# Expert weights in a mixture-of-experts stage: 96 transfers of 4 MB instead of 192 of 2 MB

## The chip, the cores and the metric

One core of one Trainium2 chip runs the whole program in one launch. The metric is the device time in microseconds of one execution; lower is better. All data is float32.

## What is computed

The reference is two network blocks, one after the other, on 256 tokens of width 1024. The first block mixes tokens with a long convolution and a gated linear scan, then runs a two-level mixture of experts. The second has two layers with five branches each (attention, recurrences, gated mixing, attention to a memory) and a wide merge. The change lies in the mixture of experts, whose core is, for every expert:

```python
def hier_moe(h, w_rg, w_re, w_gate, w_up, w_down):
    ...
    def expert_block(args):
        xe, e = args
        return (jax.nn.silu(xe @ w_gate[e]) * (xe @ w_up[e])) @ w_down[e]
    yb = lax.map(expert_block, (xb, block_eid)).reshape(n_slots, D)
    y = jnp.zeros_like(hf).at[tok_buf].add(yb * gate_buf[:, None].astype(yb.dtype))
```

There are 64 experts, of which each token uses two. One expert has a gate and an up matrix of 1024 x 512 and a down matrix of 512 x 1024. A weight is used for the few tokens that its expert gets, so all 64 experts' weights, 403 MB, have to be read once.

## The kernel before

The expert stage runs in rounds; in a round each expert takes up to 32 tokens (CAP). The 192 fetches of the profile are one round: 16 groups (NGRP) of 4 experts (GRP), 12 units to a group. A unit is 2 MB, 16 KB on each of 128 partitions (WSLOT is 4096 floats). Units 0 to 3 of a group hold the gate weights, 4 to 7 the up weights, 8 to 11 the down weights. They go through the tile `ring`, six slots of one unit (RING): unit v goes to slot (v + 2) % 6.

SyncE (SP) does nothing but wait and issue DMAs. `expert_unit` waits until the counter `unit_free` says that the slot is free, and issues the fetch of a unit; it is called 12 times for the first group and 12 times per turn of a loop for the others. `unit_free` is raised by 4 at L1405 and by 2 at L1409, when the first stage has left slots 2 to 5 and then 0 and 1, and after that by TensorE (PE) by one after the last matmul of each unit. Each slot has a semaphore of its own, `w2_in0` to `w2_in5`, for its arrivals. Behind the expert fetches in the same queue, SP issues the first three units of the next block's weights (L445), each when its slot is free.

TensorE runs, for each group:

- L1443: gathers the group's tokens by matmuls with one-hot matrices (L1880, L1884 on VectorE prepare them); L1447 are two transposes that ScalarE copies (L1588). VectorE copies the gathered tokens to `xg` (L1889).
- L1456: for each unit v of 0 to 7, a wait for the unit, then its 8 matmuls, which show as 16 records in the profile. ScalarE (L1590) and VectorE (L1891 to L1893) work on the gate product after unit 3.
- L1461: after VectorE has made `mid` (L1896), four transposes, which ScalarE copies (L1592).
- L1470: for each unit v of 8 to 11, a wait, then its matmuls. VectorE copies the result (L1899).
- L1475: scatters the result back; VectorE adds it to the tokens (L1903), and the next group's one-hot matrices follow.

What lies between the end of unit 11 and the start of the next group's unit 0 is called the boundary below; TensorE uses no weights in it. After the last group come the final norm (L243, L1913), a barrier of all engines (L1915) and the second block, whose first matmuls are L511.

Of the kernel before, what the change touches and what calls it, by code (L numbers as in the profile page):

```python
# [13 lines left out]
P = 128  # L14
# [17 lines left out]
NGRP = NE // GRP  # L32
# [13 lines left out]
WSLOT = 4096  # L46
LN_EXP = "natural_log_exp_and_others"
RING = 6
# [204 lines left out]
def build_program(nc, d, spot):  # L253

    with ExitStack() as ctx:
# [8 lines left out]
        ring = ctx.enter_context(nc.sbuf_tensor("ring", [P, RING, WSLOT], F32))  # L264
# [936 lines left out]
        def _(sp):  # L1201
# [16 lines left out]

            def expert_unit(v, g, free):

                s = (v + 2) % RING
                sp.wait_ge(sem("unit_free"), free + v + 1)
                src = d["w_experts"][bass.ds(g * 12 + v, 1), :, :].rearrange("a p n -> (a p) n")
                sp.dma_start(ring[:, s, :], src).then_inc(sem(f"w2_in{s}"), 16)


            for v in range(12):
                expert_unit(v, 0, 0)
            sp.wait_ge(sem("rounds"), 1)
            n_rounds = sp.value_load(rounds[0:1, 0:1], min_val=1, max_val=SEQ // CAP)  # L1230
            with sp.Fori(1, n_rounds * NGRP) as it:
                g = sp.snap(it % NGRP)
                for v in range(12):
                    expert_unit(v, g, it * 12)
            for u in range(RING2):
# [5 lines left out]
        def _(pe):  # L1241
# [195 lines left out]
            with pe.Fori(0, n_rounds) as r:  # L1437
                with pe.Fori(0, NGRP) as g:
# [11 lines left out]
                    for v in range(8):  # L1450
                        s = (v + 2) % RING
                        pe.wait_ge(sem(f"w2_in{s}"), it * 32 + (v // RING + 1) * 16)
                        w = ring[:, s, :].rearrange("p (k e n) -> p k e n", k=2, n=FE)
                        for k in range(2):
                            for e in range(GRP):
                                last = pe.matmul(ps[CAP * e:CAP * (e + 1), v // 4, :], xg[:, (v % 4) * 2 + k, CAP * e:CAP * (e + 1)],  # L1456
                                                 w[:, k, e, :], start=(v % 4 == 0 and k == 0), stop=(v % 4 == 3 and k == 1))
                        last.then_inc(sem("unit_free"), 1)
# [5 lines left out]
                    for v in range(8, 12):  # L1464
                        s = (v + 2) % RING
                        pe.wait_ge(sem(f"w2_in{s}"), it * 32 + (v // RING + 1) * 16)
                        w = ring[:, s, :].rearrange("p (e n) -> p e n", n=D)
# [486 lines left out]
def expert_units(gate, up, down):  # L1954
# [4 lines left out]
    out[:, 8:] = np.asarray(down).reshape(NGRP, GRP, 4, P, D).transpose(0, 2, 3, 1, 4).reshape(NGRP, 4, P, WSLOT)  # L1959
    return out.reshape(NGRP * 12, P, WSLOT)  # L1960

# [71 lines left out]
```

## Time and profile before

| | us |
|---|---|
| median of 3 runs | 2566.71 |
| lowest and highest | 2566.13, 2588.36 |
| the profiled execution | 2564.53 |
| its span | 2562.8 |
| TensorE matmul busy | 2143.2 (84%) |
| VectorE busy | 911.7 (36%) |
| q1, the queue of SP's DMAs | 585.45 MB in 43672 packets, 56.7% of 16 engines |

The profiled execution took 1.73 us more than its span; the span is what the trace covers, from the first instruction to the last. Its own time lies 2.18 us below the median of the runs. The expert stage lies between about 440 and 1397 us of the span. A row of the timeline merges consecutive instructions of one line on one engine. "PE ... [1.47 <-DMA ring<-in_w_experts]" says that TensorE sat idle for 1.47 us before this row until a fetch of expert weights had landed. SPq is SyncE's instruction queue.

### The profile page before, as it was taken

The numbers are of one execution on the slowest core, as the hardware profiler recorded it, in microseconds if no ns is written. First come the engines' busy times: TensorE is split into PE (matmuls) and PEld (weight loads), VectorE is DVE, ScalarE is ACT, GpSimd is POOL, SyncE is SP. The second block draws the span as 40 slices with busy tenths as digits, with TensorE's granted clock in tenths as the row PEclk, the third lists the DMA queues.
The fourth block names the chain that finished last, engine by engine and source line by source line (L and its number), as shares of the span: only waits on it lengthen the run. The fifth ranks groups of instructions, "written<-read, shape, count | busy, mean of one in ns | idle before, by whom it ended". The sixth has DMA issues, their size and how long they took to land. (4 is left out here: it accounts for less than half of the span.)

```text
span 2562.8 us, 25793 instructions
## 1 busy us (share of the span) xinstructions
PE 2143.2 (84%) x10250; PEld 1416.8 (55%) x10250; DVE 911.7 (36%) x1500; ACT 290.7 (11%) x650; POOL 0.2 (0%) x4
## 2 busy tenths in 40 slices
PE   6997988667666666656666999999998999999998
PEld 3583466322222222223222777778887777868887
DVE  4245452211211111121121335455553235455553
ACT  1111021000000000000001222111002122111001
POOL 0000000000000000000000000000000000000000
PEclk7997777778888888888888999999999999999999
DMA  5130005799999999999997333324445333224442
GB/s 218 66 132 1 0 1 218 335 429 423 428 429 428 428 428 429 428 428 429 429 428 320 131 132 132 113 77 172 148 148 192 138 132 126 97 98 155 160 154 82
DMA packets 45198, 592.18 MB, mean 231 GB/s; under 512 B 5463, under 2 KB 6904, under 8 KB 7928
## 3 DMA queue, kind: packets, MB, share of 16 engines
q1 hardware_dynamic: 43672, 585.45, 56.7%
q10 hardware_dynamic: 1440, 5.57, 0.6%
q8 instruction: 55, 0.90, 0.1%
q14 instruction: 31, 0.25, 0.0%
HBM read 589.95 MB, written 1.05 MB: 231 GB/s over the span
## 5 line engine op out<-in xcount | busy, mean ns | idle before, releaser
L484 PE MATMUL ps<-arena,ring 128*128 128x256 f32 x1920 | 433.8, 382 | 7.9 <-DVE arena L911 7.8
L484 PEld LDWEIGHTS ps<-arena,ring 128*128 128x128 f32 x1920 | 362.4, 191 | 61.6 <-DVE arena L911 9.1
L1456 PE MATMUL ps<-ring,arena 128*32 128x512 f32 x2048 | 261.8, 658 | 111.9 <-DMA ring<-in_w_experts 92.1
L691 PE MATMUL ps<-arena,ring 128*128 128x256 f32 x1280 | 289.2, 378 | 0.0
L1470 PE MATMUL ps<-ring,arena 128*32 128x512 f32 x1024 | 179.0, 834 | 107.6 <-DMA ring<-in_w_experts 100.8
L691 PEld LDWEIGHTS ps<-arena,ring 128*128 128x128 f32 x1280 | 241.8, 189 | 35.3 <-issue 1.0
L1456 PEld LDWEIGHTS ps<-ring,arena 128*32 128x32 f32 x2048 | 65.0, 116 | 290.7 <-issue 148.2
L1470 PEld LDWEIGHTS ps<-ring,arena 128*32 128x32 f32 x1024 | 33.5, 133 | 236.6 <-DMA ring<-in_w_experts 156.9
L1250 PE MATMUL ps<-arena,ring 128*128 128x272 f32 (+1 forms) x640 | 150.6, 398 | 2.3 <-DVE arena L1731 2.3
L697 PE MATMUL ps<-arena,ring 128*128 128x256 f32 x640 | 151.6, 378 | 0.0
L1443 PE MATMUL ps<-arena 128*128 128x128 f32 x512 | 89.4, 356 | 67.2 <-DVE arena L1884 67.2
L1113 DVE RECIPROCAL arena<-arena 128x256 f32<-128x256 f32 x80 | 140.3, 1754 | 3.0 <-DVE arena L1112 0.3
L1250 PEld LDWEIGHTS ps<-arena,ring 128*128 128x128 f32 x640 | 124.0, 194 | 31.0 <-issue 5.6
L697 PEld LDWEIGHTS ps<-arena,ring 128*128 128x128 f32 x640 | 121.0, 189 | 17.5
L1899 DVE COPY arena<-ps 128x512 f32<-128x512 f32 x32 | 20.6, 688 | 300.9 <-PE ps L1470 300.9
L1443 PEld LDWEIGHTS ps<-arena 128*128 128x128 f32 x512 | 86.4, 267 | 73.4 <-DVE arena L1884 73.4
L1112 DVE TENSOR_SCALAR arena<-arena 128x256 f32<-128x256 f32 x80 | 23.7, 296 | 176.1 <-ACT arena L876 176.1
L1475 PE MATMUL ps<-arena 128*128 128x256 f32 x256 | 65.9, 415 | 22.5 <-DVE arena L1899 22.5
L497 PE MATMUL ps<-ring,arena 128*128 128x512 f32 x192 | 84.2, 593 | 0.0
L1475 PEld LDWEIGHTS ps<-arena 128*128 128x128 f32 x256 | 51.7, 207 | 51.4 <-DVE arena L1899 43.6
L876 ACT ACTIVATE arena<-ps 128x256 f32<-128x256 f32 x80 | 30.9, 386 | 371.9 <-PE ps L691 371.9
L908 DVE RECIPROCAL arena<-arena 128x256 f32<-128x256 f32 x40 | 70.2, 1755 | 1.4
(347 smaller groups left out, 1802.7 us busy)
## 6 DMA issues: line engine op xcount, KB each, us to landing
ring<-in_w_experts SPq DMA_DIRECT2D x192, 2048.0 KB, 25.5
ring<-in_w_layers SPq DMA_DIRECT2D x44, 2048.0 KB, 7.8
ring<-in_w_layers SPq DMA_DIRECT2D x40, 1536.0 KB, 6.5
ring<-in_w_first SPq DMA_DIRECT2D x10, 2048.0 KB, 8.5
arena<-in_late ACTq DMA_DIRECT2D x2, 896.0 KB, 4.9
arena<-in_fourier SPq DMA_DIRECT2D x1, 1632.0 KB, 13.8
arena<-in_gm_rows ACTq DMA_DIRECT2D x2, 768.0 KB, 6.3
arena<-in_const SPq DMA_DIRECT2D x1, 1141.0 KB, 5.2
```

What stands on the lines that cost most here:

```text
L484: last = pe.matmul(ps[:, j % 2, 0:SEQ], t[:, s, k, :], lhs[:, k, :], start=(k == 0), stop=(k == KD - 1))
L497: last = pe.matmul(ps[:, bank_of(name, j), :], lhs[:, k, m * P:(m + 1) * P], t[:, :, k, :], start=(k == 0), stop=(k == KD - 1))
L691: last = pe.matmul(ps[:, j % 2, 0:SEQ], t[:, k, :], an[:, k, :], start=(k == 0), stop=(k == KD - 1))
L697: last = pe.matmul(ps[:, (j + 1) % 2, 0:SEQ], t[:, KD + k, :], y_all[:, n, k, :], start=(k == 0), stop=(k == 3))
L876: act.activation(esig[:, p % 2, :], ps[:, j % 2, 0:SEQ], ACT.Exp, scale=-1.0).then_inc(sem(f"job_out{j % 2}"), 1)
L908: link(dve.reciprocal(e, e))
L1113: link(dve.reciprocal(e, e))
L1250: last = pe.matmul(ps[:, j % 2, 0:n], w[:, s, k, :], rhs(k), start=(k == 0), stop=(k == KD - 1))
L1443: last = pe.matmul(ps[:, 4 + k // 4, (k % 4) * P:(k % 4 + 1) * P], xn[:, tt, k * P:(k + 1) * P], onehot[:, tt, :], start=(tt == 0), stop=( ...
L1456: last = pe.matmul(ps[CAP * e:CAP * (e + 1), v // 4, :], xg[:, (v % 4) * 2 + k, CAP * e:CAP * (e + 1)], w[:, k, e, :], start=(v % 4 == 0 a ...
L1470: last = pe.matmul(ps[CAP * e:CAP * (e + 1), 2 + half, :], mid_t[:, v - 8, CAP * e:CAP * (e + 1)], w[:, e, half * 512:(half + 1) * 512], s ...
L1475: last = pe.matmul(ps[:, 4 + k // 2, (k % 2) * SEQ:(k % 2 + 1) * SEQ], y_slot[:, k * P:(k + 1) * P], back, start=True, stop=True)
```

## The change

The host lays two consecutive units side by side for each partition: the array is 96 blocks of 128 x 8192 in place of 192 of 128 x 4096. `expert_pair` replaces `expert_unit`: it is called for v = 0, 2, ... 10, waits until both slots of the pair are free (free + v + 2 in place of free + v + 1) and fetches 4 MB into the adjoining slots s and s + 1, 32 KB on each partition. Three semaphores remain, `w2_in0` to `w2_in2`, one for each pair of slots. TensorE waits only ahead of the even units. Its matmuls, their order, the ring's 96 KB per partition and the rise of `unit_free` by one after each unit stay as they are.

```diff
--- before.py
+++ after.py
@@ -1216,22 +1216,22 @@
                     sp.wait_ge(sem("strip"), 4 * (u - RING1 + 1))
                 sp.dma_start(ring[:, u % RING1, :], d["w_first"][u]).then_inc(sem(f"w1_in{u % RING1}"), 16)
 
-            def expert_unit(v, g, free):
+            def expert_pair(v, g, free):
 
                 s = (v + 2) % RING
-                sp.wait_ge(sem("unit_free"), free + v + 1)
-                src = d["w_experts"][bass.ds(g * 12 + v, 1), :, :].rearrange("a p n -> (a p) n")
-                sp.dma_start(ring[:, s, :], src).then_inc(sem(f"w2_in{s}"), 16)
-
-
-            for v in range(12):
-                expert_unit(v, 0, 0)
+                sp.wait_ge(sem("unit_free"), free + v + 2)
+                src = d["w_experts"][bass.ds(g * 6 + v // 2, 1), :, :].rearrange("a p n -> (a p) n")
+                sp.dma_start(xr(ring[:, s:s + 2, :]), src).then_inc(sem(f"w2_in{s // 2}"), 16)
+
+
+            for v in range(0, 12, 2):
+                expert_pair(v, 0, 0)
             sp.wait_ge(sem("rounds"), 1)
             n_rounds = sp.value_load(rounds[0:1, 0:1], min_val=1, max_val=SEQ // CAP)
             with sp.Fori(1, n_rounds * NGRP) as it:
                 g = sp.snap(it % NGRP)
-                for v in range(12):
-                    expert_unit(v, g, it * 12)
+                for v in range(0, 12, 2):
+                    expert_pair(v, g, it * 12)
             for u in range(RING2):
                 sp.wait_ge(sem("unit_free"), n_rounds * (NGRP * 12) + (SLOT2[u] - 2) % RING + 1)
                 layer_unit(sp, 0, u)
@@ -1449,7 +1449,8 @@
                     pe.wait_ge(sem("xg"), 2 * it + 2)
                     for v in range(8):
                         s = (v + 2) % RING
-                        pe.wait_ge(sem(f"w2_in{s}"), it * 32 + (v // RING + 1) * 16)
+                        if v % 2 == 0:
+                            pe.wait_ge(sem(f"w2_in{s // 2}"), it * 32 + (v // RING + 1) * 16)
                         w = ring[:, s, :].rearrange("p (k e n) -> p k e n", k=2, n=FE)
                         for k in range(2):
                             for e in range(GRP):
@@ -1463,7 +1464,8 @@
                     pe.wait_ge(sem("mid_t"), it + 1)
                     for v in range(8, 12):
                         s = (v + 2) % RING
-                        pe.wait_ge(sem(f"w2_in{s}"), it * 32 + (v // RING + 1) * 16)
+                        if v % 2 == 0:
+                            pe.wait_ge(sem(f"w2_in{s // 2}"), it * 32 + (v // RING + 1) * 16)
                         w = ring[:, s, :].rearrange("p (e n) -> p e n", n=D)
                         for half in range(2):
                             for e in range(GRP):
@@ -1957,7 +1959,7 @@
     for i, w in enumerate((gate, up)):
         out[:, 4 * i:4 * i + 4] = np.asarray(w).reshape(NGRP, GRP, 4, 2, P, FE).transpose(0, 2, 4, 3, 1, 5).reshape(NGRP, 4, P, WSLOT)
     out[:, 8:] = np.asarray(down).reshape(NGRP, GRP, 4, P, D).transpose(0, 2, 3, 1, 4).reshape(NGRP, 4, P, WSLOT)
-    return out.reshape(NGRP * 12, P, WSLOT)
+    return out.reshape(NGRP * 6, 2, P, WSLOT).transpose(0, 2, 1, 3).reshape(NGRP * 6, P, 2 * WSLOT)
 
 
 def layout(a):
```

On SyncE, the first group's fetches and the head of the loop over the others (`-` before, `+` after; ISA is a wait):

```order
 L1217 DMA ring<-in_w_first 128x4096 [waits strip] x6
-L1224 DMA ring<-in_w_experts 128x4096 [waits unit_free] x12
+L1224 DMA ring<-in_w_experts 128x8192 [waits unit_free] x6
 L1230 TENSOR_LOAD rounds [waits rounds]
 L1230 ISA x2
@@ -19,38 +19,20 @@
 L1231 ISA
 L1224 ISA [waits unit_free]
-L1224 DMA ring<-in_w_experts 128x4096
+L1224 DMA ring<-in_w_experts 128x8192
 L1222 REGISTER_ALU
 L1224 ISA [waits unit_free]
```

The twelve fetches of 128 x 4096 ahead of the loop are six of 128 x 8192, and in the loop each wait stands ahead of a fetch of twice the size; the loop shrinks from twelve such steps to six.

On TensorE, the down units 8 to 11 of a group, before:

```order
L1470 MATMUL ps<-ring,arena 32x512 [waits w2_in4,mid_t]
L1470 MATMUL ps<-ring,arena 32x512 x7
L1470 MATMUL ps<-ring,arena 32x512 [waits w2_in5]
L1470 MATMUL ps<-ring,arena 32x512 x7
L1470 MATMUL ps<-ring,arena 32x512 [waits w2_in0]
L1470 MATMUL ps<-ring,arena 32x512 x7
L1470 MATMUL ps<-ring,arena 32x512 [waits w2_in1]
L1470 MATMUL ps<-ring,arena 32x512 x7
```

and after (line numbers have moved by two):

```order
L1472 MATMUL ps<-ring,arena 32x512 [waits w2_in2,mid_t]
L1472 MATMUL ps<-ring,arena 32x512 x15
L1472 MATMUL ps<-ring,arena 32x512 [waits w2_in0]
L1472 MATMUL ps<-ring,arena 32x512 x15
```

Four waits, one ahead of each unit's matmuls, have become two, and unit 9 follows unit 8, and unit 11 unit 10, with no wait between them. (The program counts 8 matmuls to a unit, the profile 16 records.)

## Rows read from the trace of the kernel before

**Rows 1.** Page, part 2: GB/s moved in each of 40 slices of 64 us.
```profile
GB/s 218 66 132 1 0 1 218 335 429 423 428 429 428 428 428 429 428 428 429 429 428 320 131 132 132 113 77 172 148 148 192 138 132 126 97 98 155 160 154 82
```

**Rows 2.** Page, part 5: the matmuls that use the expert units, gate/up and down.
```profile
L1456 PE MATMUL ps<-ring,arena 128*32 128x512 f32 x2048 | 261.8, 658 | 111.9 <-DMA ring<-in_w_experts 92.1
...
L1470 PE MATMUL ps<-ring,arena 128*32 128x512 f32 x1024 | 179.0, 834 | 107.6 <-DMA ring<-in_w_experts 100.8
```

**Rows 3.** DMA view, 600 to 1300 us: packets and what they moved.
```profile
DMA packets 20594, 299.93 MB, mean 428 GB/s; under 512 B 2288, under 2 KB 2288, under 8 KB 2288
...
q1 hardware_dynamic: 20594, 299.93, 100.6%
```

**Rows 4.** Waits of the DMA-issuing queue: total us, times, longest.
```profile
SPq L1224 <- PE ps L1456: 554.8, 126, 37.6
...
SPq L1224 <- PE ps L1470: 259.0, 60, 6.0
```

**Rows 5.** Line 1224, its DMAs: issue to landing.
```profile
DMA to landing us min/median/max: 7.7/25.5/27.2
```

**Rows 6.** Timeline at the start: start us, us, engine, line, operation, count, [idle before].
```profile
458.83 10.51 PE L1456 MATMUL ps<-ring,arena 128*32 128x512 f32 x96 [1.25 <-DVE arena L1889]
...
460.81 59.33 SPq L1224 DMA_DIRECT2D ring<-in_w_experts  x16
```

**Rows 7.** Timeline at the end of the expert stage.
```profile
1370.38 3.33 PE L1470 MATMUL ps<-ring,arena 128*32 128x512 f32 x16 [2.13 <-DMA ring<-in_w_experts]
...
1375.27 1.93 PE L1470 MATMUL ps<-ring,arena 128*32 128x512 f32 x16 [1.56 <-DMA ring<-in_w_experts]
...
1399.31 2.92 PE L511 MATMUL ps<-ring 128*128 128x512 f32 x3 [7.62 <-ACT ring L745]
```

**Rows 8.** Timeline of the boundary between groups 9 and 10.
```profile
1018.01 3.43 PE L1470 MATMUL ps<-ring,arena 128*32 128x512 f32 x16 [2.97 <-DMA ring<-in_w_experts]
...
1022.90 1.93 PE L1470 MATMUL ps<-ring,arena 128*32 128x512 f32 x16 [1.47 <-DMA ring<-in_w_experts]
...
1026.24 3.72 PE L1475 MATMUL ps<-arena 128*128 128x256 f32 x16 [1.41 <-DVE arena L1899]
...
1034.17 5.46 PE L1443 MATMUL ps<-arena 128*128 128x128 f32 x32 [4.21 <-DVE arena L1884]
...
1041.10 4.49 PE L1456 MATMUL ps<-ring,arena 128*32 128x512 f32 x39 [1.24 <-DVE arena L1889]
```

**Rows 9.** Timeline of the boundary between groups 1 and 2.
```profile
553.02 3.64 PE L1470 MATMUL ps<-ring,arena 128*32 128x512 f32 x16 [1.25 <-DMA ring<-in_w_experts]
...
558.08 6.78 PE L1475 MATMUL ps<-arena 128*128 128x256 f32 x16 [1.41 <-DVE arena L1899]
...
576.97 4.50 PE L1456 MATMUL ps<-ring,arena 128*32 128x512 f32 x40 [1.24 <-DVE arena L1889]
```

**Rows 10.** Windows: busy us (count) of PE, PEld, DVE, ACT, POOL, PEclk, DMA, GB/s.
```profile
545.00:564.00 19.00, 14.54 (x54) 5.96 (x47) 1.29 (x2) 0.00 (x0) 0.00 (x0) 0.50 1.01 429
...
1039.00:1052.00 13.00, 9.65 (x88) 3.23 (x87) 4.39 (x4) 0.97 (x2) 0.00 (x0) 1.00 1.01 431
```

**Rows 11.** Waits of VectorE at the boundaries, 400 to 1360 us.
```profile
DVE arena L1889 <- PE ps L1443: 90.9, 16, 6.5
...
DVE arena L1903 <- PE ps L1475: 64.7, 15, 6.9
```

**Rows 12.** DMA view, 1398 to 1412 us: small packets alone.
```profile
DMA packets 576, 2.11 MB, mean 151 GB/s; under 512 B 64, under 2 KB 192, under 8 KB 576
...
q10 hardware_dynamic: 576, 2.11, 40.8%
```

**Rows 13.** DMA view, 14 to 34 us: packets of mixed size, back to back.
```profile
DMA packets 671, 8.60 MB, mean 430 GB/s; under 512 B 74, under 2 KB 74, under 8 KB 148
...
q1 hardware_dynamic: 671, 8.60, 101.8%
```

## The prediction

> **What bounds the kernel now.** I read four views. First, the page's slices of moved bytes [rows 1]: from slice 9 on, for twelve slices of 64 us, the core moves 423 to 429 GB/s, and nowhere else as much. That plateau is the expert stage. Second, the page's groups [rows 2]: TensorE's unit matmuls (L1456, L1470) are busy 261.8 and 179.0 us in all, and sat idle 92.1 and 100.8 us ahead of them until a fetch had landed. So TensorE waits for weights, not the other way round. Third, the DMA view of 700 us inside the plateau [rows 3]: the 16 engines' packets fill 100.6% of their time. No engine pauses, so in this stage the end is set by bytes and by time per byte. Fourth, SyncE's waits [rows 4]: it stands still until TensorE frees a slot, 126 and 60 times, yet the engines never run dry, since about five older fetches are in flight: a fetch lands 25.5 us (median) after its issue [rows 5], and one follows another by 4.89 us (1370.38 to 1375.27, [rows 7]).
>
> The stream runs from the first refill, issued at 460.81 [rows 6], to the last landing at about 1375.2 [rows 7]: 186 units (192 less the six fetched in advance) in 914 us. After it comes a serial tail to the second block's first matmul at 1399.31 [rows 7], which moves with it.
>
> **The change, part by part.** The bytes stay. Changed are the size of a packet, the moment at which a fetch may start, and the moment at which TensorE may begin.
>
> 1. Packets. A partition's row is one packet: [rows 3] has 20594 packets less 2288 completion markers, 18306 for 299.93 MB, which is 16.4 KB each. With rows of 32 KB, each of 16 engines moves 8 packets for 4 MB where it moved 16, so 8 fixed costs per pair go, in 93 streamed pairs. The trace has no 32 KB packet. From one side: in [rows 12], 512 data packets of 4.1 KB take 0.408 x 16 x 14 us = 91.4 us, 178 ns each; in [rows 3], 1.006 x 16 x 700 us / 18306 = 615 ns each. The slope is 437 ns over 12.26 KB, and the line meets zero bytes at 32 ns. This is too high for a stream, because transfers that start from rest are in it. It bounds the gain at 93 x 8 x 32 ns = 24 us. From the other side: in [rows 13], back to back, 597 data packets averaging 14.4 KB moved 430 GB/s, no less than the 428 of full 16 KB rows, so nothing is seen to be lost to packets: gain 0. The stream resembles the second far more, so I take a quarter of the first, 8 ns: 6.0 us gained. A loss from larger rows is a rival below.
>
> The Trainium skill's "DMA: Bandwidth & Descriptors" (Where 436 GB/s comes from) gives the fabric's ceiling as 435 GB/s; the 428 of [rows 3] are 1.6% below it. If all of that were fixed cost per packet, an estimate from that page, halving the packets would give back 0.8% of 914 us, 7.5 us, in place of 6.0. Packets of 32 KB are not in the trace.
>
> 2. Start. SyncE now waits for two freed units. 96 records, six units, take 10.51 us [rows 6], 1.75 us a unit at the full clock. The first refill goes out after the second unit in place of the first: +1.7 us. The stream has no slack to take it back. The four units issued ahead (L1405) and the two behind (L1409) were free at the same moments anyway.
>
> 3. End. Unit 10 was consumed while unit 11 was under way; now both land together. TensorE starts 32 records after the last landing in place of 16. One unit costs 1.75 us at full clock and 3.3 to 3.6 us at half [rows 7, 9]: +1.7 to +3.5, I take +2.5. The next block's first fetches, queued on SyncE behind the experts, also wait for units 6, 10 and 11 of the last group. The last of these is freed 2 us after the last landing and a lone 2 MB takes 7.7 us [rows 5], so the first is there well before the 1399.31 of L511, and later ones are needed later: 0.
>
> 4. The boundary between groups is the place at risk. While TensorE is between unit 11 and the next group's unit 1, only the fetches in flight feed the engines. Let pair 5 (units 10, 11) land at time 0. Pairs 0, 1 and 2 of the next group then last for 3 x 9.79 = 29.4 us. The next fetch goes into pair 0's slots, so TensorE must have finished unit 1 of the next group before that, less the time from a freed slot to moving bytes. For this time 7.7 us for a lone fetch less 4.9 us of transfer gives at most 2.8 us [rows 5, 7]. Between groups 9 and 10 [rows 8], from the start of unit 11 at 1022.90 to unit 0 at 1041.10 are 18.2 us, plus two units, 3.7 us: 21.9. Pairing adds unit 10 in front, 1.7 to 3.3 us: 23.6 to 25.2. With 2.8 that is 26.4 to 28.0, inside 29.4: no stall. Between groups 1 and 2 [rows 9] it is 23.95 + 3.7 = 27.6, with unit 10 29.3 to 30.9, and with the latency up to 33.7: a stall of 0 to 4.3 us, I take 1.9. The difference is TensorE's clock. In [rows 10] the slow boundary's first part is at a granted 0.50, which is 1.2 GHz, and a later stretch at 1.00, 2.4 GHz; the scatter took 6.78 us against 3.72 [rows 8, 9]. How many boundaries are slow? VectorE's waits [rows 11] average 64.7/15 = 4.31 us for the scatter and 90.9/16 = 5.68 for the gather, against 3.88 and 5.56 at the fast one (its matmul time plus about 0.1). Summed, that is about 8 us of excess, of which the slow boundary has 4. So I count one stalled boundary of 15: +1.9.
>
> In the kernel before, the same six units in flight, 29.4 us, stood against a shorter chain, which ended with unit 0: 18.2 + 1.9 = 20.1 us, or 25.9 at the slow boundary [rows 8, 9]. That is why [rows 1] shows no dip there.
>
> Inside a group TensorE consumes a pair in 3.5 to 7 us of each 9.79, so it is never behind, and the two waits removed per pair save nothing while it waits for the same bytes. SyncE issues half as many fetches of about 0.3 us each; it was idle: 0.
>
> Sum: -6.0 + 1.7 + 2.5 + 1.9 = +0.1 us. On the profiled execution that is 2564.53 + 0.1 = 2564.6. That run lies 2.2 us below the median of runs, 2566.71; on the median it is 2566.8, my forecast.
>
> **The rivals.**
>
> - Larger rows bring nothing per byte, because the descriptors are cut to 16 KB again or their fixed cost is hidden. The change then doesn't do what it says for the packets. For it: [rows 13]. Against it: the slope of [rows 12]. Then -6.0 falls away: 2566.8 + 6.0 = 2572.8.
> - Every boundary stalls (the other side). TensorE's work is the same, but comes in bursts after gaps of 4 to 6 us, where it was spread in gaps of 3. If it enters every boundary at 1.2 GHz, the 15 chains look like [rows 9]: 15 x 1.9 = 28.5 us in place of 1.9, which gives 2593.4. It decides from the point where the chain plus latency passes 29.4 us. For it: units already take 3.4 us after a gap of 2.97 us [rows 8]. Against it: in that same row the chain was fast all the same, and the scatter after it ran at 3.72.
> - The rate falls. 16 engines read rows that lie 32 KB apart in place of 16 KB; if their reads met in the memory more often, the plateau itself would sink. Each percent costs 9.1 us; 3% give 2566.8 + 27.4 = 2594.2. Nothing in the trace shows it. The same page of the Trainium skill (Latency and other measured facts) reports copies with power-of-two row pitches losing rate, 207 GB/s at a pitch of 512 KiB and 103 at 4 MiB, with 214 as the full rate; no row here has such a pitch.
> - The fixed cost is really the 32 ns of [rows 12]: -24 in place of -6.0, 2548.8.
>
> **How the numbers follow.** The forecast has 0.69, no gain per packet 0.15, all boundaries 0.08, a falling rate 0.03, the large gain 0.03, and 0.02 are for what I did not think of. About 1% (26 us) is what a measurement of this kernel can tell from no change. Faster by over 1% would need more than the whole upper bound of the gain: 0.02. Slower by over 1% takes the second or third rival, of which a tenth may be milder: 0.10. Within 1%: 0.88. The range: below, 12 ns a packet (3.0 less), no stall (1.9 less), an end at full clock (0.8 less) and the profiled run's lower base (2.2 less) give 2558.9, say 2558. Above, no gain per packet (6.0 more), three boundaries stalled in place of one (3.8 more) and an end at half clock (1.0 more) give 2577.6, say 2578.
>
> **What would show it.** In the profile after: q1 with 12288 data packets and 1536 completion markers fewer (about 29850 in place of 43672), each expert row as one packet of about twice the duration; a plateau of 428 to 431 GB/s; the first refill at about 462.5; the last landing near 1373 and L511 at about 1399.4; TensorE's idle time before L1457 and L1472 in half as many pieces of twice the length. A DMA share under 100% in any stretch of the plateau is a boundary stall, with one pair's fetch landing more than 9.8 us after the one before. It would be wrong if the packets stay at 16 KB, if the rate drops, or if dips come in every group.

## The result, and the profile after

The changed kernel is slower, by about half a percent. Over 20 runs of each, the ratio of its runs to those of the kernel before is 1.0053, with a 95% interval of 1.0028 to 1.0079; the medians are 2597.94 and 2583.98 us. The runs of either kernel lie at two levels 18 to 20 us apart, for a reason ahead of the expert stage (last section), so times are compared here level with level: lower level 2580.2 against 2566.7 in the mean (7 and 6 runs), upper level 2600.2 against 2584.9. That is +13.5 and +15.3 us. The profiled execution took 2579.68 us, its span is 2577.9, against 2564.53 and 2562.8. The forecast was +0.1, on a median of three runs (2566.71) that equals the mean of the lower six, and its range ended at 2578.

| | before | after |
|---|---|---|
| profiled execution, us | 2564.53 | 2579.68 |
| first unit's matmul | 458.83 | 458.57 |
| first refill issued | 460.81 | 462.27 |
| last landing used by TensorE | 1375.27 | 1385.78 |
| second block's first matmul | 1399.31 | 1414.45 |
| expert stage, first unit to second block | 940.5 | 955.9 |

The whole loss lies in the expert stage: +15.4 us there, +15.1 in the span.

The page of the changed kernel: GB/s in 40 slices, the packets of q1, and the two groups of unit matmuls. They answer to [rows 1] and [rows 2].

```profile
GB/s 217 65 131 1 0 1 217 348 424 416 427 418 429 422 428 430 416 430 427 422 422 298 160 131 112 99 109 150 159 157 168 160 131 111 98 110 150 158 158 82
...
q1 hardware_dynamic: 29848, 585.45, 56.3%
...
L1457 PE MATMUL ps<-ring,arena 128*32 128x512 f32 x2048 | 261.2, 667 | 132.5 <-DMA ring<-in_w_experts 112.6
...
L1472 PE MATMUL ps<-ring,arena 128*32 128x512 f32 x1024 | 171.9, 832 | 111.8 <-DMA ring<-in_w_experts 111.8
```

q1 has 29848 packets, as was expected of 32 KB rows. The twelve slices of the plateau, 423 to 429 in [rows 1], now run from 416 to 430: some are as high as before and some lower. TensorE's idle time ahead of the unit matmuls until a fetch had landed rose from 92.1 + 100.8 to 112.6 + 111.8 us.

The DMA view of the changed kernel for the same 700 us as in [rows 3]. Its GB/s row has 40 slices of 17.5 us.

```profile
GB/s 421 448 410 427 442 403 433 427 440 376 442 419 423 431 438 412 418 433 429 421 433 431 410 438 431 434 374 446 423 418 423 444 418 421 436 433 389 446 423 403
DMA packets 10196, 296.88 MB, mean 424 GB/s; under 512 B 1136, under 2 KB 1136, under 8 KB 1136
...
q1 hardware_dynamic: 10196, 296.88, 99.3%
```

The mean fell from 428 to 424 GB/s and the engines' share from 100.6% to 99.3%: they now pause. In the fine row the low values (410, 403, 376, 374, 389) come back about once in three or four slices, once to a group.

The timeline at both ends of the stage, which answers to [rows 6] and [rows 7]:

```profile
458.57 10.51 PE L1457 MATMUL ps<-ring,arena 128*32 128x512 f32 x96 [1.25 <-DVE arena L1891]
...
462.27 7.20 SPq L1224 DMA_DIRECT2D ring<-in_w_experts  x3
...
1385.78 6.57 PE L1472 MATMUL ps<-ring,arena 128*32 128x512 f32 x32 [6.00 <-DMA ring<-in_w_experts]
...
1414.45 5.95 PE L511 MATMUL ps<-ring 128*128 128x512 f32 x8 [7.61 <-ACT ring L745]
```

The first refill goes out 3.7 us after the first matmul, in place of 2.0: the late start of 1.7 us, as predicted. From the last landing to the second block are 28.67 us in place of 24.04: a late end of 4.6 us, where 2.5 were predicted.

The boundary between groups 0 and 1, which answers to [rows 8]:

```profile
495.55 6.24 PE L1472 MATMUL ps<-ring,arena 128*32 128x512 f32 x32 [4.28 <-DMA ring<-in_w_experts]
...
503.21 3.72 PE L1477 MATMUL ps<-arena 128*128 128x256 f32 x16 [1.42 <-DVE arena L1901]
...
511.18 5.40 PE L1443 MATMUL ps<-arena 128*128 128x128 f32 x32 [4.25 <-DVE arena L1886]
...
518.04 10.51 PE L1457 MATMUL ps<-ring,arena 128*32 128x512 f32 x96 [1.24 <-DVE arena L1891]
...
536.51 0.20 PEld L1457 LDWEIGHTS ps<-ring,arena 128*32 128x32 f32 x8 [8.87 <-DMA ring<-in_w_experts]
```

Units 10 and 11 landed at 495.55, and unit 1 of the next group was done at about 518.04 + 3.64 = 521.7, so the chain is 26.1 us long, 0.9 above the 23.6 to 25.2 predicted for a boundary at full clock. Yet the refill, pair 3, was usable only at 536.51, which is 40.96 us after pair 5. Four transfers at 9.71 us (a sixth of 58.28, the group without dips measured below) take 38.85. The stream lost 2.1 us. Windows around this boundary and the next show where (busy us of the engines, then the granted TensorE clock, the DMA share, GB/s; a packet is counted, with its time and its bytes, in the window in which it starts):

```profile
515.00:521.00 6.00, 4.76 (x45) 2.53 (x47) 1.29 (x2) 0.37 (x1) 0.00 (x0) 1.00 1.00 431
521.00:523.00 2.00, 2.00 (x24) 0.67 (x20) 0.00 (x0) 0.00 (x0) 0.00 (x0) 1.00 0.97 328
523.00:525.00 2.00, 2.00 (x24) 0.59 (x20) 0.00 (x0) 0.00 (x0) 0.00 (x0) 1.00 0.62 229
525.00:531.00 6.00, 3.55 (x36) 0.87 (x28) 4.48 (x3) 0.60 (x1) 0.00 (x0) 1.00 1.01 431
...
581.00:583.00 2.00, 2.00 (x24) 0.58 (x20) 0.00 (x0) 0.00 (x0) 0.00 (x0) 1.00 0.08 33
```

Up to 521 the engines run at 431 GB/s. Then follow 328 and 229, with a share of 0.62 in the last, and at 525 all run again. From 521 to 523 the share is still 0.97 at only 328 GB/s, so the packets that start there take about a quarter longer than those before. At the next boundary two microseconds hold 33 GB/s. A dip stands in every one of the 15 boundaries, but they are unequal in depth.

VectorE's waits in the boundaries, as in [rows 11]:

```profile
DVE arena L1891 <- PE ps L1443: 98.6, 16, 6.9
...
DVE arena L1905 <- PE ps L1477: 62.1, 16, 3.9
```

62.1/16 = 3.9 us for the scatter says that TensorE's clock was at 2.4 GHz in all 16 scatters. The slow boundary on which the prediction laid its whole stall did not come back; the stalls came without it.

A measure that needs no ends: from the landing of units 10 and 11 of group 0 (495.55) to that of group 15 (1385.78) are 15 groups of 59.35 us. Before, unit 11 landed at 494.29 and 1375.27: 58.73 us a group. I call this the group period below; where units 10 and 11 land one after the other it is taken from unit 11. Before, every group takes 58.7 or 58.8 us. In the changed kernel single groups take 58.3 to 60.4 us, and 59.35 is their mean.

### The profile page after: what moved, and what is told of

Its sections match the earlier page's. It is cut to its first block and busy times, and to the rows that moved or that the text cites. A ratio compares the mean times of both kernels' runs of the same rounds, so it can differ in the third digit from the quotient of the medians.

```text
span 2577.9 us, 25427 instructions
## 1 busy us (share of the span) xinstructions
PE 2129.9 (83%) x10250; PEld 1428.8 (55%) x10250; DVE 912.0 (35%) x1500; ACT 290.7 (11%) x650; POOL 0.2 (0%) x4
## 3 DMA queue, kind: packets, MB, share of 16 engines
q1 hardware_dynamic: 29848, 585.45, 56.3%
HBM read 589.95 MB, written 1.05 MB: 229 GB/s over the span
## 5 line engine op out<-in xcount | busy, mean ns | idle before, releaser
L1457 PE MATMUL ps<-ring,arena 128*32 128x512 f32 x2048 | 261.2, 667 | 132.5 <-DMA ring<-in_w_experts 112.6
L1472 PE MATMUL ps<-ring,arena 128*32 128x512 f32 x1024 | 171.9, 832 | 111.8 <-DMA ring<-in_w_experts 111.8
L1457 PEld LDWEIGHTS ps<-ring,arena 128*32 128x32 f32 x2048 | 69.5, 121 | 312.7 <-issue 176.7
L1472 PEld LDWEIGHTS ps<-ring,arena 128*32 128x32 f32 x1024 | 43.4, 145 | 229.1 <-issue 142.4
L1443 PE MATMUL ps<-arena 128*128 128x128 f32 x512 | 97.1, 376 | 67.2 <-DVE arena L1886 67.2
L1113 DVE RECIPROCAL arena<-arena 128x256 f32<-128x256 f32 x80 | 140.3, 1754 | 3.0 <-DVE arena L1112 0.3
L697 PEld LDWEIGHTS ps<-arena,ring 128*128 128x128 f32 x640 | 121.0, 189 | 17.5
L1477 PE MATMUL ps<-arena 128*128 128x256 f32 x256 | 59.5, 385 | 22.7 <-DVE arena L1901 22.7
L1898 DVE TENSOR_TENSOR arena<-arena,ps 128x512 f32<-128x512 f32 x16 | 11.0, 690 | 178.0 <-PE ps L1457 178.0
```

The source lines that it names most:

```text
L697: last = pe.matmul(ps[:, (j + 1) % 2, 0:SEQ], t[:, KD + k, :], y_all[:, n, k, :], start=(k == 0), stop=(k == 3))
L1113: link(dve.reciprocal(e, e))
L1443: last = pe.matmul(ps[:, 4 + k // 4, (k % 4) * P:(k % 4 + 1) * P], xn[:, tt, k * P:(k + 1) * P], onehot[:, tt, :], start=(tt == 0), stop=( ...
L1472: last = pe.matmul(ps[CAP * e:CAP * (e + 1), 2 + half, :], mid_t[:, v - 8, CAP * e:CAP * (e + 1)], w[:, e, half * 512:(half + 1) * 512], s ...
L1477: last = pe.matmul(ps[:, 4 + k // 2, (k % 2) * SEQ:(k % 2 + 1) * SEQ], y_slot[:, k * P:(k + 1) * P], back, start=True, stop=True)
```

## The experiments

Theory A: the queues run dry at every boundary, because with pairs the first refill after it needs unit 10, unit 11, the boundary, unit 0 and unit 1 one after the other. Theory B: rows of 32 KB, or the layout that goes with them, are slower by themselves. Theory A2: one of the two coarse waits is enough by itself. For each kernel the table gives the stage (first unit's matmul to the second block's first, from the timeline), the group period, the mean rate from 600 to 1300 us, and the ratio to the kernel before with its interval.

| kernel | stage us | group period us | GB/s | ratio to before |
|---|---|---|---|---|
| before | 940.5 | 58.73 | 428 | |
| after | 955.9 | 59.35 | 424 | 1.0053 (1.0028 to 1.0079) |
| e_both | 959.4 | 59.67 | 421 | 1.0081 (1.0048 to 1.0114) |
| e_sp_pair | 943.7 | 58.76 | 428 | 1.0016 (0.9986 to 1.0046) |
| e_pe_pair | 944.7 | 58.77 | 428 | 1.0015 (0.9987 to 1.0043) |
| e_layout | 941.8 | 58.73 | 428 | 0.9997 (0.9968 to 1.0025) |
| e_after_twice | 990.4 | 61.45 | 410 | 1.0209 (1.0157 to 1.0262) |
| e_before_twice | 947.5 | 58.97 | 426 | 1.0032 (0.9997 to 1.0067) |
| e_split | 937.5 | 58.44 | 431 | 0.9989 (0.9960 to 1.0018) |
| e_split6 | 939.0 | 58.37 | 431 | 1.0001 (0.9979 to 1.0023) |
| e_split10 | 936.3 | 58.37 | 431 | 0.9995 (0.9964 to 1.0026) |
| e_hoist | 938.0 | 58.28 | 432 | 1.0014 (0.9987 to 1.0041) |
| e_hoist_before | 940.1 | 58.72 | 429 | 0.9977 (0.9952 to 1.0002) |
| e_hoist_split10 | 935.7 | 58.36 | 431 | 0.9916 (0.9886 to 0.9946) |

Most differences here are smaller than the spread of the runs, so the stage and the period decide; each is read from one profiled run.

**The waits without the large transfer (e_both).** The kernel before with both waits made coarse; layout and fetches of 2 MB stay.

```diff
-                sp.wait_ge(sem("unit_free"), free + v + 1)
+                sp.wait_ge(sem("unit_free"), free + v + 2 - v % 2)
...
-                        pe.wait_ge(sem(f"w2_in{s}"), it * 32 + (v // RING + 1) * 16)
+                        if v % 2 == 0:
+                            pe.wait_ge(sem(f"w2_in{s}"), it * 32 + (v // RING + 1) * 16)
+                            pe.wait_ge(sem(f"w2_in{s + 1}"), it * 32 + (v // RING + 1) * 16)
```

> The kernel before with its layout and its 2 MB fetches of 16 KB rows, but SyncE waits for both slots of a pair ahead of the first of its two fetches, and TensorE waits for both units of a pair ahead of the first. Theory A (the queues run dry at each boundary, since the chain from the landing of a pair to the freeing of the next pair's slots is too long): the same dips as in the changed kernel, about 0.6 us of idle engines and as much of slow restart in each of 15 boundaries, and without the gain of larger packets: 2564.5 + 13.6 + 6 = about 2584, last landing near 1391. Rival B (32 KB rows or the layout are slower by themselves): no loss but the later start and end, 2564.5 + 4 = 2569.

Measured: 2581.97 us in the profiled run, stage 959.4, period 59.67, units 10 and 11 of the last group in use at 1388.56. The DMA view, 600 to 1300 us:

```profile
GB/s 430 429 407 432 428 422 432 427 429 425 432 427 403 433 428 409 428 432 428 390 431 426 404 430 432 427 400 433 426 411 433 430 390 423 430 426 368 432 432 398
DMA packets 20252, 294.86 MB, mean 421 GB/s; under 512 B 2256, under 2 KB 2256, under 8 KB 2256
```

The same dips without any 32 KB row: ten slices between 368 and 411, and none that low in between. The loss against before is 18.9 us of stage, more than the changed kernel's 15.4, since the larger packets are missing. Theory B is not needed for the dips, and e_hoist below rules it out. The size of the step from this kernel to the changed one is 3.5 us where 6 were expected; at the dips the two differ, so this pair doesn't give the packets' gain cleanly.

**One wait at a time (e_sp_pair, e_pe_pair).** e_sp_pair has the first of the two edits above alone, e_pe_pair the second alone.

> The kernel before; only SyncE's wait is changed: ahead of an even unit's fetch it waits for both slots of the pair. TensorE still takes each 2 MB unit as it lands. Theory A: the chain lacks unit 10 in front, 1.7 to 3.3 us, so it is about 22 to 24 us against 29.4; fewer or no dips, +1.7 for the later start and 0 to 3 for dips: 2566 to 2569. Rival A2 (the wait for two free slots is enough by itself to run the queues dry): +12 or more, 2577 or more. Rival B: 2566.

> The kernel before; only TensorE's waits are changed: it waits for both units of a pair ahead of the first. SyncE still refills each slot as it is freed. Theory A: the chain ends with unit 0 and not unit 1, so it is 1.7 us shorter than in the changed kernel, about 23.5 to 25; few dips: +2.5 at the end and 0 to 4 for dips, 2567 to 2571. Rival A2 (late consumption alone causes the loss): 2577 or more. Rival B: 2567.

Measured: stage 943.7 and 944.7, +3.2 and +4.2 us, with no loss in the period (58.76 and 58.77). The DMA views, 600 to 1300 us, of e_sp_pair and then of e_pe_pair:

```profile
DMA packets 20594, 299.93 MB, mean 428 GB/s; under 512 B 2288, under 2 KB 2288, under 8 KB 2288
...
q1 hardware_dynamic: 20594, 299.93, 100.7%
```

```profile
DMA packets 20587, 299.82 MB, mean 428 GB/s; under 512 B 2288, under 2 KB 2288, under 8 KB 2288
...
q1 hardware_dynamic: 20587, 299.82, 100.7%
```

Rate and share are those of [rows 3] (100.7% in place of 100.6%). So neither wait runs the queues dry by itself. What they cost lies at the ends of the stage. Theory A2 falls. It takes both, because each lengthens the same chain, one in front and one behind. Measured from the landing of the last bytes of a group, with the means over 15 boundaries read from the unit matmuls: in e_pe_pair the slot wanted first is free after 24.3 us (unit 0), in e_sp_pair after 23.0 (unit 1, with unit 10 out of the way), and nothing is lost; in the changed kernel it is free after 26.0 (25.1 to 26.6), and 1.07 us a group are lost in the mean; in e_both it is free after 26.1, and 0.94 are lost (59.67 - 58.73).

**The layout alone (e_layout).** Units are fetched singly out of the paired blocks: rows of 16 KB at a pitch of 32 KB.

```diff
-                src = d["w_experts"][bass.ds(g * 12 + v, 1), :, :].rearrange("a p n -> (a p) n")
+                src = d["w_experts"][bass.ds(g * 6 + v // 2, 1), :, (v % 2) * WSLOT:(v % 2 + 1) * WSLOT].rearrange("a p n -> (a p) n")
...
-    return out.reshape(NGRP * 12, P, WSLOT)
+    return out.reshape(NGRP * 6, 2, P, WSLOT).transpose(0, 2, 1, 3).reshape(NGRP * 6, P, 2 * WSLOT)
```

> The kernel before with the new layout in memory only: two units side by side for each partition, and each unit still fetched alone, 16 KB rows at a pitch of 32 KB, all waits as before. Theory A: nothing changes, 2564.5 in a profiled run, packets of 612 ns. Rival B (the pitch of 32 KB costs rate): packets longer than 612 ns or the plateau under 428 GB/s, each percent 9.1 us; to explain the whole loss it takes about 1.5 to 2 percent, 2578 to 2584.

```profile
DMA packets 20594, 299.93 MB, mean 428 GB/s; under 512 B 2288, under 2 KB 2288, under 8 KB 2288
...
q1 hardware_dynamic: 20594, 299.93, 100.6%
```

Packets, bytes and share are word for word those of [rows 3], and the period is 58.73. The pitch costs nothing. The stage is 1.3 us longer than before all the same, and its last unit shows why:

```profile
1373.05 3.54 PE L1470 MATMUL ps<-ring,arena 128*32 128x512 f32 x16 [2.98 <-DMA ring<-in_w_experts]
```

It took 3.54 us where the last unit before took 1.93 [rows 7]; the granted clock in it was 0.53, against 1.00. From the last landing to the second block are 25.7 us here, and in e_sp_pair too, against 24.0 before. So the end of the kernel before was 1.6 us shorter than that of two kernels whose TensorE waits in the same way.

**A longer boundary (e_after_twice, e_before_twice).** The scatter's matmuls are issued twice; the second pass writes the same values.

```diff
-                    for k in range(KD):
+                    for k in [*range(KD), *range(KD)]:
                         last = pe.matmul(ps[:, 4 + k // 2, (k % 2) * SEQ:(k % 2 + 1) * SEQ], y_slot[:, k * P:(k + 1) * P], back,
```

> The changed kernel with the scatter matmuls of every group done twice (the second overwrites the same result), which lengthens each of 15 boundaries and the tail by 3.7 us at full clock. Theory A: the boundary already decides the stream, so nearly all of it is added to the time: 16 x 3.7 = 59 us, at least 45, over the changed kernel: about 2625 to 2640. Rival B (the rate or the ends cost the 13 us, and the boundary has slack): only the last group's 3.7 us, about 2584.

> The kernel before with the scatter matmuls of every group done twice, 3.7 us more in each boundary. Its chain of 20.1 us (25.9 at a slow boundary) becomes 23.8 to 29.6 against 29.4 less the latency and the lead of the fast engines. Theory A: little slack used up, dips at slow boundaries only, 3.7 us for the last group and 0 to 10 for dips: 2568 to 2578. If before had no slack either: 59 us, 2623.

e_after_twice, the boundary between groups 1 and 2, timeline and windows:

```profile
557.75 6.30 PE L1472 MATMUL ps<-ring,arena 128*32 128x512 f32 x32 [5.98 <-DMA ring<-in_w_experts]
...
565.47 7.17 PE L1477 MATMUL ps<-arena 128*128 128x256 f32 x32 [1.42 <-DVE arena L1901]
...
583.75 10.51 PE L1457 MATMUL ps<-ring,arena 128*32 128x512 f32 x96 [1.24 <-DVE arena L1891]
...
599.84 0.20 PEld L1457 LDWEIGHTS ps<-ring,arena 128*32 128x32 f32 x8 [6.50 <-DMA ring<-in_w_experts]
```

```profile
580.00:586.00 6.00, 4.76 (x46) 3.06 (x48) 1.29 (x2) 0.37 (x1) 0.00 (x0) 0.98 0.95 410
586.00:588.00 2.00, 2.00 (x24) 0.59 (x20) 0.00 (x0) 0.00 (x0) 0.00 (x0) 1.00 0.00 0
588.00:590.00 2.00, 2.00 (x24) 0.68 (x20) 0.00 (x0) 0.00 (x0) 0.00 (x0) 1.00 0.95 262
```

The chain is now 29.6 us (557.75 to about 587.4), no packet starts from 586 to 588, and the refill can be used 12.4 us after unit 1 is done (599.84). This is the plain case, and all 15 boundaries are alike. It gives the time from a freed slot to a usable lone pair: 12.4 us, of which 9.7 are the transfer. The profiled run took 2614.64 us; the stage grew by 34.5 us where 45 to 59 were expected. The direction is theory A's, the size is not: the period grew by 2.10 us for a chain that grew by 3.6. So in the changed kernel the boundary was not past the limit; it sat just inside it. 26.0 + 12.4 = 38.4 us against 4 x 9.7 = 38.8 for four transfers back to back: by these two numbers alone there should have been no loss at all, and it lost 1.07 us a group. The difference lies in the refill: from the end of unit 1 to the usable refill, the changed kernel took 12.4 to 14.9 us, 14.0 in the mean, where e_after_twice took 12.4. In e_before_twice the period grew by 0.24 us only, and two of the 15 groups, at 60.7 and 60.4 us, make up nearly all of that. The kernel before had room for 3.7 us more in most of its boundaries.

**Halves where they matter (e_split, e_split6, e_split10).** Chosen pairs are fetched as two halves with a semaphore each, the others as 4 MB: units 6 and 7, which take the slots freed first after a boundary, and units 10 and 11, which land last ahead of it.

```diff
+            SPLIT = (6, 10)
+            def expert_half(v, g, free):
+                s = (v + 2) % RING
+                sp.wait_ge(sem("unit_free"), free + v + 1)
+                src = d["w_experts"][bass.ds(g * 6 + v // 2, 1), :, (v % 2) * WSLOT:(v % 2 + 1) * WSLOT].rearrange("a p n -> (a p) n")
+                sp.dma_start(ring[:, s, :], src).then_inc(sem(f"w2_half{v % 2}_{v // 2}"), 16)
...
-                        if v % 2 == 0:
-                            pe.wait_ge(sem(f"w2_in{s // 2}"), it * 32 + (v // RING + 1) * 16)
+                        if v - v % 2 in (6, 10):
+                            pe.wait_ge(sem(f"w2_half{v % 2}_{v // 2}"), it * 16 + 16)
+                        elif v % 2 == 0:
+                            pe.wait_ge(sem(f"w2_pair{v // 2}"), it * 16 + 16)
```

> The changed kernel, but of each group's six pairs, two are fetched as two halves of 2 MB with semaphores of their own: units 6 and 7, which refill the slots freed first after a boundary, and units 10 and 11, which land last ahead of it. The other four pairs stay single fetches of 4 MB with 32 KB rows. Theory A: no dips, no late start and no late end, and two thirds of the gain of larger packets: 2564.5 - 4 = about 2560. Rival B (32 KB rows are slower): two thirds of the loss stays, 2573.

> The changed kernel, but units 6 and 7 of each group are fetched as two halves of 2 MB, each into its slot as soon as that is freed; the other five pairs stay single fetches. Units 10 and 11 still land together. The stage is counted from the first unit's matmul to the second block's first (940.5 us before, 955.9 in the changed kernel). Theory A: the refill after a boundary now hangs on unit 0 alone, 24.3 us after the landing of units 10 and 11, as in the kernel with only TensorE's waits paired, where nothing ran dry. So no dips and no late start, the late end of 4.7 us stays, and five sixths of 7.0 us are gained: 939.4. Rival (the late landing of unit 10 is enough for part of the dips): 943 or more.

> The changed kernel, but units 10 and 11 of each group are fetched as two halves of 2 MB with a semaphore each, so that TensorE takes unit 10 while unit 11 is under way; the other five pairs stay single fetches, and the refill after a boundary still waits for units 0 and 1. Theory A: the chain from unit 11 to unit 1 is about 23 us, no dips, no late end, the late start of 1.7 stays, five sixths of 7.0 us gained: stage 936.4. Rival (waiting for two free slots is enough for part of the dips): 943 or more.

Measured stages of e_split, e_split6 and e_split10: 937.5, 939.0 and 936.3; the last two were expected at 939.4 and 936.4. e_split's is 3.0 us under before, where 4 were expected. The DMA view of e_split10, 600 to 1300 us:

```profile
DMA packets 12086, 301.67 MB, mean 431 GB/s; under 512 B 1344, under 2 KB 1344, under 8 KB 1344
...
q1 hardware_dynamic: 12086, 301.67, 100.3%
```

No dips, and more bytes in 700 us than in either given kernel (301.67 MB, against 299.93 and 296.88). Splitting either pair is enough: the slot wanted first is free 24.2 us after the landing of units 10 and 11 in e_split6, and 23.3 us after that of unit 11 in e_split10. e_split10 is the better one, since it also takes away the late end.

**A shorter boundary (e_hoist, e_hoist_before, e_hoist_split10).** All fetches of e_hoist stay those of the changed kernel. The next group's one-hot matrices, its gather and the copy to `xg` move from the boundary to the place after `mid`, where TensorE waits for the down weights; only the first group's stand ahead of the loop. The core of the edit on TensorE:

```diff
+                gather(pe.snap(r * (NGRP + 1) + 1))
                 with pe.Fori(0, NGRP) as g:
                     it = pe.snap(r * NGRP + g)
-                    pe.wait_ge(sem("onehot"), it + 1)
-                    for k in range(KD):
-                        ...
-                    last.then_inc(sem("gather_ps"), 1)
+                    pe.wait_ge(sem("scattered"), it * 4 + 4)
...
                     last.then_inc(sem("mid_ps"), 1)
+                    gather(nx + 2)
```

> The changed kernel with all its 4 MB fetches; the one-hot matrices and the gather of the next group are moved from the boundary to ahead of the down units, where TensorE waits for weights, and only scatter, addition and two transposes stay in the boundary. Its length falls from 16.2 us to about 8. Theory A: the queues no longer run dry, the plateau is 431 GB/s without dips, and the loss of the changed kernel goes: 2580 - 15 = about 2563 to 2567. Rival B: no change against the changed kernel, 2579.

> The kernel before (2 MB fetches into six slots) with the next group's one-hot matrices and gather moved ahead of the down units, as in the changed kernel with the moved gather, which brought 17.9 us to the stage there. Theory A: before has no dry queues, so a shorter boundary buys it almost nothing: 940.5 less 0 to 2 us for the tail. Rival (the moved gather is faster by itself, whatever the queues do): a gain of 10 us or more, 930 or less.

> The changed kernel with both the gather moved out of the boundary and units 10 and 11 fetched as two halves. Theory A: no dips, no late end, late start of 1.7 us, five sixths of the gain of larger packets: about 938.0 - 4.7 + 1.2 = 934.5 for the stage, 6 us under the kernel before; in a profiled run 2558 to 2560.

e_hoist, the boundary between groups 1 and 2, and its DMA view:

```profile
555.40 5.57 PE L1480 MATMUL ps<-ring,arena 128*32 128x512 f32 x32 [5.10 <-DMA ring<-in_w_experts]
...
562.39 3.72 PE L1485 MATMUL ps<-arena 128*128 128x256 f32 x16 [1.42 <-DVE arena L1922]
...
569.12 5.34 PE L1464 MATMUL ps<-ring,arena 128*32 128x512 f32 x32
```

```profile
DMA packets 10374, 302.19 MB, mean 432 GB/s; under 512 B 1152, under 2 KB 1152, under 8 KB 1152
...
q1 hardware_dynamic: 10374, 302.19, 100.3%
```

From the landing at 555.40 to the end of unit 1 (569.12 + 5.34) are 19.1 us, the plateau is 432 GB/s, and the period 58.28, the lowest of all. The stage fell from 955.9 to 938.0. The same edit on the kernel before left the stage at 940.1 against 940.5: there was nothing in the boundary to gain while the queues never ran dry. e_hoist_split10 came out at 935.7 (expected 934.5). Its ratio, 0.9916 (0.9886 to 0.9946), is the only one clear below 1, but it overstates the gain: compared as in the section on the result, the means are 2557.0 against 2565.3 (5 and 6 runs) and 2576.5 against 2584.1 (2 and 24 runs), so about 8 us. Some 5 of these are from the stage. The part behind the stage, whose code is the same, took 1158.5 us in its profiled run and 1162.6 to 1164.1 in the 13 others; the cause of that is open.

## Why the prediction was wrong

**What bounds the kernel: right.** The stream sets the end of the stage, and the loss is a loss of the stream.

**Packets: right, a little better than priced.** The period without dips is 58.28 us (e_hoist) against 58.73: 0.45 us a group, times 15.5 groups of streamed fetches, is 7.0 us, where I took 6.0. Per packet saved that is 0.45/48, 9 ns, where I took 8; e_hoist_before shows that the moved gather has no share in it (58.72). The estimate of 7.5 us by the Trainium skill's "DMA: Bandwidth & Descriptors" (Where 436 GB/s comes from) came out close. The 432 GB/s of e_hoist lie 0.7% below the 435 GB/s that this page of the Trainium skill gives as the ceiling.

**Start: right.** +1.7 us between first matmul and first refill; +1.5 by the end of group 0.

**End: right in kind, too small.** 4.6 us in place of 2.5. Units 10 and 11 end 6.6 us after the landing, against 1.9 for unit 11 before: the granted clock was 0.50 in unit 10, which took 3.4 us, and 0.61 in unit 11. The forecast laid a slow clock on unit 10 alone. And 1.6 us of the 4.6 are chance of the base: in e_layout and e_sp_pair the last unit ran at about half clock too, and against their end the changed kernel's is 3.0 us longer.

**The boundary: the step that failed.** The prediction had the right place and the right limit (29.4 less 2.8, measured 29.1 less 2.7), and then counted "one stalled boundary of 15: +1.9". Measured, the 15 boundaries lost 15 x (59.35 - 58.28) = 16.1 us, 1.07 each in the mean and between nothing and 2.1 one by one. The sum of the parts is 16.1 - 7.0 + 1.7 + 4.6 = 15.4, the stage's loss.

The chain came out too short as well: 23.6 to 25.2 us were forecast at full clock, 26.0 is the mean (25.1 to 26.6). The boundary of [rows 8], on which it was built, is one of the shortest of before. From the start of unit 11 to unit 0 it has 18.2 us, where the mean of all 15 is 19.6, because unit 11 took 2.8 to 3.6 us in 9 of them and not 1.9. VectorE's waits [rows 11], by which the slow boundaries were counted, do not contain unit 11. But this alone does not give the loss: with the chain as measured the prediction's own sum is 26.0 + 2.7 = 28.7 us against 29.1, still no stall, and not even the longest chain, 26.6, passes the limit by more than 0.2.

The wrong step was to take the queue as one thing that is full until a moment and empty after it, so that a chain inside the limit costs nothing. The stream is 16 engines that are not in step. The first dip shows it. Each engine reports its share of a transfer by itself, and the trace has these completions: for the pair ahead of the dip, 14 lie at 522.5 to 523.1 us and two at 524.6 and 524.7. By the trace's packets, the 14 engines ran out between 522.1 and 522.7, and the refill issued at 521.9 gave them their first packets at 522.9 to 523.7, while the two still moved old data until 524.2. For the refill, 15 completions lie at 533.4 to 534.4 and one at 536.5. TensorE gets a pair when the last engine has landed it, so a landing says how late the last engine is and hides how early the others will run out. The limit is therefore soft, and begins some microseconds before the sum says.

Idle time is only the larger half of the loss. Those 14 first packets took 1.4 to 2.2 us each, where the others take 1.2. Over 600 to 1300 us the changed kernel has 9060 data packets in 99.3% of the engines' time, 1227 ns each, and e_hoist 9222 in 100.3%, 1218 ns: 48 packets a group make 0.45 us of longer packets, and the missing point of share is 0.6 us of idle engines, together 1.05 of the 1.07. One engine also came out of the first dip 2.1 us behind the rest, and TensorE waits for that one. That the engines' being out of step is what softens the limit is my reading of these events; no run varied it by itself, and why a refill that comes just in time takes longer than one into empty queues stays open. The loss of a single boundary does not follow its chain either: with 26.6 us one group took 58.4 us and another 60.4. What the runs do show is the limit's place: no loss at mean chains of 23.0, 24.2 and 24.3 us, 1.07 us a group at 26.0, 3.17 at 29.6.

The slow boundary was the wrong worry. I took the one boundary at 1.2 GHz [rows 9] for the only candidate. After the change the clock was at 2.4 GHz in every scatter, and the dips came all the same.

**The rivals.** "Every boundary stalls" is what happened, but by a softer limit at full clock and not by a slow clock; I gave it 0.08, and priced at 1.9 us a boundary it would have been 2593. "Larger rows bring nothing" and "the rate falls" are ruled out by e_layout and e_hoist, and the 32 ns a packet of the last rival by the 9 measured. The page of the Trainium skill named there (Latency and other measured facts) reports losses for large power-of-two row pitches; here 32 KB against 16 KB costs nothing (58.73 us a group in both), which says nothing of the larger pitches named there. The change of 0.5% stays inside the band of 1% that had 0.88, but lies above the range, whose upper end allowed for three stalled boundaries and not for fifteen.

## What to carry to other kernels

When transfers are merged, both of their ends get coarser: the consumer starts later and the slots come back later, and where both lie in one chain their delays add. Compare that chain with what is in flight and leave a few microseconds, not just a positive remainder (here 2.2 us of slack, 26.4 less the 24.2 of e_split6, cost nothing, and 0.4 us, 26.4 less 26.0, cost 1.07 us a group). Merge only the transfers that don't stand at the ends of such a chain: here, one split pair out of six kept most of the gain (58.37 us a group in e_split6 and e_split10, between 58.73 and 58.28) and lost nothing.

## What the runs showed of the hardware

- Halving the packets of a full stream saved about 9 ns for each packet that went (0.45 us for 48 per engine and group), far below the 32 ns that short transfers from rest suggested. Six completion markers per engine and group, of 9 ns each in the trace, went with them and are in this figure.
- The first packets after an idle moment are slow: 14 packets of 32 KB at 522.9 to 523.7 us took 1.4 to 2.2 us, where those of the full stream take 1.2.
- A lone pair of 4 MB could be used 12.4 us after its slot was free, 2.7 us more than its transfer, in all 15 boundaries of e_after_twice.
- TensorE's clock in a stage ahead of the experts differs between executions and moves everything behind it by some 20 us. Of the 14 profiled runs, 8 have a granted clock of 0.81 between 300 and 350 us, and their first unit starts at 456.9 to 460.5; 6 have 0.57, and theirs starts at 477.6 to 480.6. In the profiled run of the kernel before and in that of e_sp_pair, whose code is the same up to there, the windows from 300 to 350 us and a group of matmuls in them:

```profile
300.00:350.00 50.00, 45.08 (x184) 26.67 (x183) 27.62 (x59) 7.35 (x20) 0.00 (x0) 0.81 0.00 0
...
L1324 PE MATMUL ps<-arena,ring 128*128 128x272 f32 (+1 forms) x96 | 30.6, 467 | 5.4 <-DVE ring L1710 5.4
```

```profile
300.00:350.00 50.00, 47.40 (x125) 24.97 (x124) 18.15 (x38) 2.55 (x7) 0.00 (x0) 0.57 0.00 0
...
L1324 PE MATMUL ps<-arena,ring 128*128 128x272 f32 (+1 forms) x96 | 39.9, 580 | 5.4 <-DVE ring L1710 5.4
```

The granted clock is 0.81 in the one and 0.57 in the other, the same 96 records take 30.6 and 39.9 us, and the first unit starts at 458.8 and 477.8. TensorE worked in short pieces between waits there in both; what tips the clock one way or the other was not tried. For differences of a few microseconds the stage's own length is the better measure than the time of a run.
